# Expert up projections of a mixture-of-experts layer: 448-column matmuls over high and low halves, summed when the bank is emptied

## The reference, cut to what matters

```python
def swiglu(h, w1, w3, w2):
    return jnp.einsum('btf,fd->btd', jax.nn.silu(jnp.einsum('btd,df->btf', h, w1)) * jnp.einsum('btd,df->btf', h, w3), w2)

def moe_swiglu(h, router_w, w1, w3, w2):
    ...
    for e in range(N_EXPERTS):
        y = y + gates[..., e:e + 1] * swiglu(h, w1[e], w3[e], w2[e])
```

## Time and profile before

| what | value |
|---|---|
| median of 3 runs | 2365.25 us (2361.47 to 2369.6) |
| time of the profiled execution | 2361.21 us |
| span of its trace | 2359.4 us |
| TensorE busy, share of the span | 90% |
| VectorE busy | 52% |
| ScalarE busy | 29% |
| mean granted TensorE clock | 0.952 |

### The profile page before, as it was taken

The page is one execution under the profiler, slowest core; times in us unless marked ns, Lnnn a source line. Parts: engine busy times, 40 slices in busy tenths (PEclk is TensorE's granted clock), DMA queues, the critical chain, the costliest instruction groups (busy, mean ns, idle before and its releaser), DMA issues.

```text
span 2359.4 us, 48492 instructions
## 1 busy us (share of the span) xinstructions
PE 2134.6 (90%) x20724; PEld 1854.9 (79%) x20724; DVE 1217.7 (52%) x2472; ACT 687.4 (29%) x1177; POOL 283.1 (12%) x390
## 2 busy tenths in 40 slices
PE   6999887889899999999999887889869999999996
PEld 6656566886699999999657667886669988889885
DVE  4656764544466323323656663543245665666653
ACT  1111223331322122122111233331124444444442
POOL 0000315530000000000000224520000110100101
PEclk8999989999899999999999889999869999999998
DMA  6444201001124422210534201000065566656654
GB/s 236 142 161 127 92 3 41 4 4 37 59 89 139 137 78 72 72 55 18 178 127 141 78 3 41 4 4 1 0 220 203 182 203 194 209 196 210 205 172 140
DMA packets 185710, 252.32 MB, mean 107 GB/s; under 512 B 8065, under 2 KB 136785, under 8 KB 185329
## 3 DMA queue, kind: packets, MB, share of 16 engines
q1 hardware_dynamic: 180000, 232.85, 29.3%
q0 software_dynamic: 5504, 16.39, 3.0%
HBM read 235.07 MB, written 16.78 MB: 107 GB/s over the span
## 4 chain that ended last, share of the span: by engine, by line
PE 83%; DVE 8%; issue 3%; ACT 2%; POOL 2%; DMA 1%; SPq 0%; DVEq 0%; POOLq 0%; ACTq 0%
PE bank L923 42%; PE bank L914 11%; PE bank L1180 8%; PE bank L1422 6%; PE bank L1059 3%; PE bank L875 2%; PE bank L896 2%; PE bank L1148 1%; PE bank L1136 1%; PE bank L1165 1%; DVE arena L2260 1%; DVE rms L1878 1%; PE bank L1449 1%; ACT arena L1582 1%; DVE arena L2164 1%
## 5 line engine op out<-in xcount | busy, mean ns | idle before, releaser
L923 PE MATMUL bank<-g_hi,w_hi 128*128 128x224 f32 (+1 forms) x1376 | 396.5, 288 | 38.6 <-DVE g_lo L2008 38.5
L923 PE MATMUL bank<-g_lo,w_hi 128*128 128x224 f32 (+1 forms) x1376 | 395.1, 287 | 0.0
L923 PE MATMUL bank<-g_hi,w_lo 128*128 128x224 f32 (+1 forms) x1376 | 393.8, 286 | 0.0
L1180 PE MATMUL bank<-arena 64*64 64x64 f32 (+1 forms) x8640 | 268.9, 229 | 45.5 <-issue 17.4
L1180 PEld LDWEIGHTS bank<-arena 64*64 64x64 f32 x8640 | 252.8, 137 | 60.1 <-issue 36.3
L923 PEld LDWEIGHTS bank<-g_hi,w_hi 128*128 128x128 f32 x1376 | 267.9, 195 | 40.6 <-DVE g_lo L2008 40.2
L914 PE MATMUL bank<-arena,ring 128*128 128x320 f32 (+1 forms) x1024 | 287.6, 440 | 10.0 <-ACT arena L1582 10.0
L1993 DVE TENSOR_TENSOR w_lo<-ring,w_hi 128x1024 fp32r<-128x1024 f32 x192 | 230.8, 1223 | 112.3 <-ACT w_hi L1805 109.1
L923 PEld LDWEIGHTS bank<-g_lo,w_hi 128*128 128x128 f32 x1376 | 268.1, 195 | 0.0
L923 PEld LDWEIGHTS bank<-g_hi,w_lo 128*128 128x128 f32 x1376 | 267.9, 195 | 0.0
L914 PEld LDWEIGHTS bank<-arena,ring 128*128 128x128 f32 (+1 forms) x1024 | 191.6, 189 | 94.6 <-issue 13.7
(11 more groups left out here) (274 smaller groups left out, 2884.9 us busy)
## 6 DMA issues: line engine op xcount, KB each, us to landing
ring<-in_moe_w SPq DMA_DIRECT2D x96, 1024.0 KB, 7.2
arena<-in_mod_w SPq DMA_DIRECT2D x32, 1024.0 KB, 5.3
ring<-in_ffn_w SPq DMA_DIRECT2D x30, 1024.0 KB, 7.9
ring<-in_mod_w SPq DMA_DIRECT2D x16, 1024.0 KB, 7.3
ring<-in_w_in SPq DMA_DIRECT2D x16, 1024.0 KB, 8.2
ring<-in_w_out SPq DMA_DIRECT2D x8, 1024.0 KB, 9.1
ring<-in_dft SPq DMA_DIRECT2D x4, 1024.0 KB, 7.0
ring<-in_w_in SPq DMA_DIRECT2D x4, 896.0 KB, 11.5
```

Of the source, the lines that this page charges most:

```text
L923: ins = mm(out, lhs[x], rhs[y], start=(first and i == 0), stop=(last and i == 2))
L1180: return mm(out[HD * col:HD * col + HD], lhs[HD * r:HD * r + HD], rhs[HD * r:HD * r + HD], start=first, stop=last, skip_group_check=not (f ...
```

## The change

The high and low rows are now two halves of one tensor, `g_both`. For each `kt` the high weights meet both in one matmul of 2 x 224 = 448 columns: columns 0 to 223 collect high x high, columns 224 to 447 high x low. The third product (low weight x high rows) is added into the first half. So a unit is 8 pairs of matmuls in place of 24 matmuls, and fills a bank of its own. The two halves are summed when the bank is emptied: ScalarE copies the second half to SBUF (`e_part`), VectorE adds the first half to it and frees the bank. This is done for q = 0 (into `e_sil`) and q = 1 (into `e_up`). Silu and the product then work from SBUF. Each addition is followed by a drain of VectorE.

```
         GW = 6144
-        g_hi, g_lo = sbr("g_hi", GW), sbr("g_lo", GW)
+        g_both = sbr("g_both", 2 * GW)
+        g_hi, g_lo = g_both[:, 0:GW], g_both[:, GW:2 * GW]
...
+        xg_both = g_both[:, :].rearrange("p (s n) -> p s n", s=2)
+        e_up, e_part = view(silt, 2 * CAP, CAP), view(silt, 3 * CAP, 2, CAP)
...
                                 for q in range(2):
+                                    b = psum[o.open(pe, ("up", k, f, q), it)]
                                     w = unit(EXP_UNITS * k + 2 * f + q, KT, P)
                                     for kt in range(KT):
...
-                                        ins = split3(b[:, CAP * q:CAP * q + CAP], [x[:, kt, :] for x in w],
-                                                     [x[:, kt, :] for x in xg], kt == 0, kt == KT - 1)
-                                    if q == 0:
-                                        ins.then_inc(s_used2, 1)
-                                end2(ins)
+                                        mm(b[:, 0:2 * CAP], w[0][:, kt, :], xg_both[:, :, CAP * kt:CAP * kt + CAP],
+                                           start=(kt == 0), stop=False, skip_group_check=True)
+                                        ins = mm(b[:, 0:CAP], w[1][:, kt, :], xg[0][:, kt, :],
+                                                 start=False, stop=(kt == KT - 1), skip_group_check=True)
+                                    end2(ins)
...
@@ scalar
-                                        b = take2(("up", k, c))
-                                        if c >= 2:
-                                            act.wait_ge(s_glo2, u - 1)
-                                        ac(e_sil[:, c % 2, :], b[:, 0:CAP], ACT.Silu).then_inc(s_sil2, 1)
-                                        o.wait_emptied(act, ("up", k, c), it)
+                                        for q in range(2):
+                                            b = take2(("up", k, c, q))
+                                            ac(e_part[:, q, :], b[:, CAP:2 * CAP], ACT.Copy).then_inc(s_upcopy, 1)
+                                        act.wait_ge(s_upsum, 2 * u + 1)
+                                        ac(e_sil[:, c % 2, :], e_sil[:, c % 2, :], ACT.Silu).then_inc(s_sil2, 1)
+                                        act.wait_ge(s_upsum, 2 * u + 2)
                                         ac(eg[0][:, c, 0:CAP], e_sil[:, c % 2, :], ACT.Copy).then_inc(s_ghi2, 1)
...
@@ vector
-                                    b = take2(("up", k, c))
+                                    for q, dst in enumerate((e_sil[:, c % 2, :], e_up)):
+                                        b = take2(("up", k, c, q))
+                                        ve.wait_ge(s_upcopy, 2 * u + q + 1)
+                                        end2(v.tensor_tensor(dst, b[:, 0:CAP], e_part[:, q, :], ALU.add))
+                                        ve.drain()
+                                        if q == 0:
+                                            ve.sem_inc(s_upsum, 1)
                                     ve.wait_ge(s_sil2, u + 1)
-                                    end2(v.tensor_tensor(e_sil[:, c % 2, :], b[:, CAP:2 * CAP], e_sil[:, c % 2, :], ALU.mult))
+                                    v.tensor_tensor(e_sil[:, c % 2, :], e_up, e_sil[:, c % 2, :], ALU.mult).then_inc(s_upsum, 1)
                                     ve.wait_ge(s_ghi2, u + 1)
```

More of the change, by code:

```diff
@@ L280, in list_pair_groups @@
                     order.add(("sl", 1 - k, q), "V")
-            order.add(("up", k, f), "V")
+            for q in range(2):
+                order.add(("up", k, f, q), "V")
         for i in range(2):
@@ L629, in build @@
         s_rmax, s_rexp, s_rounds = sem("router_max"), sem("router_exp"), sem("rounds_ready")
-        s_moe_done = sem("experts_done")
+        s_moe_done, s_upsum, s_upcopy = sem("experts_done"), sem("up_summed"), sem("up_copied")
         s_ring2 = [sem(f"pair_ring_in{i}") for i in range(2)]
@@ L639, in build @@
         s_ca, s_cv, s_cp = sem("scalar_chain"), sem("vector_chain"), sem("pool_chain")
-        USED_SIGNALS = EXP_F + 2 * 3
+        USED_SIGNALS = 2 * 3
         block = ctx.enter_context(nc.Block())
@@ L1006, in experts @@
                                     slots(1 - k)
-                                b = psum[o.open(pe, ("up", k, f), it)]
                                 for q in range(2):
+                                    b = psum[o.open(pe, ("up", k, f, q), it)]
                                     w = unit(EXP_UNITS * k + 2 * f + q, KT, P)
@@ L1536, in wait_unit_used @@
             k, x = divmod((u - 4) % (2 * EXP_UNITS), EXP_UNITS)
-            if x < 2 * EXP_F and x % 2 == 1:
-                order2.wait_filled(eng, ("up", k, x // 2), it, back)
+            if x < 2 * EXP_F:
+                order2.wait_filled(eng, ("up", k, x // 2, x % 2), it, back)
             elif x >= 2 * EXP_F and x % 4 == 3:
@@ L1541, in wait_unit_used @@
             else:
-                before = x // 2 if x < 2 * EXP_F else EXP_F + (x - 2 * EXP_F) - (x - 2 * EXP_F) // 4
+                before = (x - 2 * EXP_F) - (x - 2 * EXP_F) // 4
                 eng.wait_ge(s_used2, (it + 1 - back) * 2 * USED_SIGNALS + k * USED_SIGNALS + before + 1)
```

## The result

The changed kernel takes 2378.73 us in the median of 7 runs (2374.08 to 2383.74), the kernel before 2365.25 us: a ratio of 1.0064, 95% interval 1.0045 to 1.0082. I had forecast 2353 us, with a range of 2336 to 2369, and had given slower a chance of 0.12. The profiled execution takes 2377.04 us, its span is 2375.2 us.

A forecast was written before the change was run, and what follows sets the result against it. TensorE, busy for 90% of the span, was taken to set the pace within an expert. Gains of 1.55 us in each of 8 experts gave 12.4 us: 2365.25 - 12.4 = 2353 us, range 2336 to 2369.

The forecast's parts named there:

- TensorE's gain: Experts' up units on TensorE: each shrinks from 2.712 to 2.498 us, 27.5 us over 128 units if TensorE never waits.
- The estimate of 2.6 us: Up matmuls on TensorE: fewer matmuls of the same columns save only 2.5 ns each, 2.6 us in all.
- the other one, from its LDWEIGHTS section: Up matmuls: a 107 ns weight load is covered by 448 columns, not by 224; 27 ns go for each `kt`.
- Rival 3: Up matmuls: no gain on TensorE, two pieces paid as two streams or columns alone count; 2365 or 2363 us, chance 0.08.
- The turn of ScalarE and VectorE: The two engines' loop for each `f` in the experts: 5.32 us a turn after, against TensorE's 5.00.
- Rivals 1 and 2: Experts' ScalarE/VectorE turn: 1, near 5.0 us, 2338 us, chance 0.18; 2, longer, 2377 us at 0.5 us more, slower chance 0.12.
- TensorE waits for `w_lo` of unit 17: Second down unit of each expert: TensorE waits about 1.9 us for VectorE's split, 8 times.
- A wait ahead of the slots: Between up and down units: if TensorE's new wait stands also there, the loop is longer than counted and the prediction fails slow.
- The wait for the selection: VectorE's selection ahead of the slots: done 0.1 us before TensorE wants it.
- At nothing: Effects priced at zero: bank openings, moved signals, row DMAs; the start of an expert untouched, its low clock noise.
- net gain of 12.4 us inside the experts: Experts' stage: 1.55 us gained an expert after TensorE's wait for unit 17, 12.4 us over 8 experts.

The follow-up runs named there:

- e5_preload: The changed kernel with a tiny Silu ahead of each pair's first expert's up steps, loading the Silu table early: 2376.9 us, ratio 1.0036 to the kernel before.
- e1_pad112: The kernel before with 56 empty VectorE drains added at step c = 10 of each expert: 2377.4 us, ratio 1.0047.
- e4_light_pad: e3_light with 24 empty VectorE drains added at step c = 10 of each expert: 2363.7 us, ratio 1.0004 to the kernel before.
- e3_light: The changed kernel without VectorE's filled-bank wait, and without the drain and signal after each addition (one drain follows both): 2356.0 us, ratio 0.9967 to the kernel before.
- e6_all: e3_light with the gate rows moved to c = 8 and the Silu table loaded early: 2360.6 us, ratio 0.9964 to the kernel before.
- e7_all_reorder: e6_all with VectorE splitting the gathered rows before w_lo of units 1 and 2 at an expert's start: 2328.6 us, ratio 0.9853 to the kernel before.
- e8_before_reorder: The kernel before with VectorE splitting the gathered rows before w_lo of units 1 and 2 at an expert's start: 2344.8 us, ratio 0.9932.

## Why the prediction was wrong, step by step

**TensorE's gain: right in kind, but 8 us smaller.** Start to start, a 448-column matmul holds TensorE for 0.21 us and the 224-column one behind it for 0.10. Timeline of TensorE before and after:

```profile
2059.85 0.28 PE L923 MATMUL bank<-g_hi,w_hi 128*128 128x224 f32 x1
2059.96 0.28 PE L923 MATMUL bank<-g_lo,w_hi 128*128 128x224 f32 x1
2060.07 0.27 PE L923 MATMUL bank<-g_hi,w_lo 128*128 128x224 f32 x1
2060.19 0.27 PE L923 MATMUL bank<-g_hi,w_hi 128*128 128x224 f32 x1
```

```profile
1995.16 0.38 PE L1017 MATMUL bank<-g_both,w_hi 128*128 128x448 f32 x1
1995.38 0.27 PE L1019 MATMUL bank<-g_both,w_lo 128*128 128x224 f32 x1
1995.48 0.38 PE L1017 MATMUL bank<-g_both,w_hi 128*128 128x448 f32 x1
1995.69 0.26 PE L1019 MATMUL bank<-g_both,w_lo 128*128 128x224 f32 x1
1995.79 0.38 PE L1017 MATMUL bank<-g_both,w_hi 128*128 128x448 f32 x1
```

The pair takes 0.316 us (I had 0.199 + 0.113 = 0.312) in place of 0.335 for the three matmuls before. I had 0.339: I divided the 21.70 us of a chain piece by 192, and these hold the way of the last matmul to the end and a slower first unit too. From unit to unit it is 2.53 us after and 2.68 before (I had 2.498 and 2.712). So 0.15 us x 128 = 19.2 us can be gained, not 27.5, as the experts without low clock and waits say (2.4 us x 8). The estimate of 2.6 us that I had taken from the Trainium skill (TensorE: Matmul & The Clock Gate, Back-to-back issue gap) is refuted by this; the other one, from its LDWEIGHTS section, 27 ns for each `kt`, comes nearer to the 19 ns measured. Rival 3 is out.

**The turn of ScalarE and VectorE: right.** Timeline of VectorE after, one turn:

```profile
2018.53 0.39 DVE L2035 TENSOR_TENSOR silu<-silu 128x224 f32<-128x224 f32 x1 [0.17 <-issue]
...
2020.33 2.36 DVE L1998 TENSOR_TENSOR w_lo<-ring,w_hi 128x1024 fp32r<-128x1024 f32 x2 [0.56 <-ACT w_hi L1809]
2022.61 0.39 DVE L2030 TENSOR_TENSOR silu<-bank,silu 128x224 f32<-128x224 f32 x1
2023.30 0.39 DVE L2030 TENSOR_TENSOR silu<-bank,silu 128x224 f32<-128x224 f32 x1 [0.30 <-issue]
2023.86 0.39 DVE L2035 TENSOR_TENSOR silu<-silu 128x224 f32<-128x224 f32 x1 [0.17 <-issue]
```

From product to product 5.33 us; I had 5.32. Rivals 1 and 2, a shorter and a longer turn, are both out: the slow side came true by another mechanism than the rival's. The waits after:

```profile
PE bank L927 <- DVE w_lo L1998: 7.5, 7, 1.6
...
PE bank L1003 <- DVE select L1945: 4.0, 4, 1.0
```

TensorE waits for `w_lo` of unit 17 as forecast, 1.3 to 1.6 us in five experts and 0.4 in two (forecast 1.9 in all eight). A wait ahead of the slots I had named as the sign of a longer loop; it came, and the loop was not longer. The wait for the selection I had put at 0.1 us to the good. I missed that in the first expert of each pair the table load stands between copy and Silu. Timeline of ScalarE after:

```profile
2069.23 0.36 ACT L1826 ACTIVATE silu<-bank 128x224 f32<-128x224 f32 x1 [1.23 <-PE bank L1019]
2069.60 1.28 ACT L1828 ACT_TABLE_LOAD   x1
2070.90 0.39 ACT L1828 ACTIVATE silu<-silu 128x224 f32<-128x224 f32 x1
```

Before, the same load ran while ScalarE waited for the bank. Now it makes the first turn 1.1 us longer, and three of the four waits ahead of the slots were followed by 3.4 us at the lower clock level. With the load out of the way (`e5_preload`) TensorE waited as long in all, at unit 17.

**The step that failed** is, first, the paragraph "At nothing": "The start of an expert ... is not touched. Low clock there comes and goes by a few us between executions; that is noise on both kernels." I counted the 32 additions, drains and waits as time of VectorE and not as length of its loop. Their length costs 7.9 us at three jumps (`e1_pad112`: 7.7 with nothing else changed; `e4_light_pad` against `e3_light`: 7.65). This and the clock took the time out of my range; the second failed step, TensorE's gain, is the 8.3 us above. The Trainium skill (Runtime: NRT & Kernel Launch, Instruction fetch mechanics) says it: "A taken branch whose target isn't in the current 2-page window forces a DMA fetch of the target page before execution can continue". The runs agree: 338 recorded instructions run without packets in the later turns of the loop, 386 with 5 in a turn, and 2.7 to 3.0 us pass behind the jump in place of 0.3.

**And the clock is not noise here.** Before, the changes of expert over the jump had TensorE's idle time in two pieces, 1.7 to 1.8 and 2.0 to 2.2 us, with the transposes between, and none of the three was followed by the lower level. After, TensorE idles 6.5 to 6.8 us in one piece there, and each time 6.8 us at 1.2 GHz begin within it. It isn't this one execution alone: the mean granted clock is 0.942 over the 7 runs after and 0.948 over 31 before, which is about 278 and 248 us at the lower level in a run (span x 2 x (1 - clock)). Part of this comes from TensorE itself. Its own jump, before and after (duration in ns, minimum, median, maximum; the last of the four leaves the loop):

```profile
L972 PEldq COMPARE_BRANCH  x4: 83/5490/5560, 1898.4 to 2334.0; - x4
```

```profile
L976 PEldq COMPARE_BRANCH  x4: 83/216/242, 1900.7 to 2350.1; - x4
```

The old loop of TensorE was itself too long for a jump without a fetch (q8: 171 packets before, 139 after), and it held back the transposes by 1.7 to 1.8 us. In the trace ten packets came in a turn of it, and none in a later turn of the new loop. The shorter loop of the change removed that stall, and gained nothing from it, since VectorE ended the wait (5.8 to 5.9 us a change in `e3_light`, as before). It only joined two short idle times into one of 4.1 us (`e3_light`, `e6_all`), behind which the clock falls for 6.8 us. That this joining is the cause is read from the traces; no run here brought TensorE's stall back. That the low clock hangs on TensorE's idle time is shown for the changes inside a turn: 3.5 us in one piece was followed by the lower level in 31 of 32 cases in eight kernels, 1.3 us (`e7_all_reorder`, `e8_before_reorder`) in none of 8. But the length of the idle time isn't all: at the jumps of `e8_before_reorder` TensorE idles less than in the kernel before, 1.8 to 1.9 us ahead of the transposes and nothing behind them, and 3.4 us at the lower level follow all three, where the kernel before had none. What decides between these is open.

**The sum, as it should have been**, in the changed kernel's stage: 19.2 us gained on TensorE; 11.5 us of its waits inside the experts (7.5 for `w_lo`, 4.0 ahead of the slots); 7.9 us at the jumps; 10.8 us by the clock. That is 11.0 us slower, against 13.6 measured. Most of the 2.6 us between lie around the same waits, because the profile counts idle time only from a matmul's modelled end: unit 16 takes 4.15 us where TensorE waits 1.26 us at its end and 2.74 where it doesn't wait, and unit 17 then 2.85 in place of 2.72. So my net gain of 12.4 us inside the experts was 4.9 us, and the 18.7 us of jump and clock, put at nothing, came on top. That half of the busy time at the lower level is lost is itself checked: in `e1_pad112`, where no matmul changed, it gives 7.2 us, and the experts' own times grew by 6.7. Over the 31 runs of the kernel before, whose time at the lower level differs by chance, a run is 0.32 us longer for each us of it: less than half, since part of it falls into idle time.

## What to carry to other kernels

In a device loop count the instructions that an edit adds to each engine's body, waits on register values and drains included, and look in the page's instruction queues whether packets for that engine come in each turn: the price is paid at the jump, where every engine may be waiting for that one. Look at what stands next to a stage's idle time before calling it untouched; two idle times that grow together can cost the clock of the work behind them. Take the price of a matmul from start to start, not from the length of a piece divided by its count. A gain on the busiest engine of 19 us was real here, and visible only when the other engines' turn and program were made shorter too.

## What the runs showed of the hardware that I had not expected

- Program length alone, 386 recorded VectorE instructions in a loop in place of 274, costs 2.5 us a jump, and up to 14 us of a stage with its effect on the clock; 338 cost nothing.
- A 448-column stream in two pieces of 224 takes 0.215 us start to start, more than the line through 320 and 512 gives (0.199), while the 224-column matmul behind it takes 0.101 us; before, one took 0.112.
- A drain and then two waits on register values held VectorE's next instruction back by 0.30 us (timeline of VectorE above), a drain and one such wait by 0.17.
